# Dilated attention of a hybrid decoder step: pieces of one query block and four key blocks for both heads, set between half tiles of the projections

## What is computed

```python
def combine_branches(outs, lses):
    wts = jax.nn.softmax(jnp.stack(lses), axis=0)
    y = sum(wts[i][..., None] * outs[i] for i in range(len(outs)))

def dilated_prompt(q, k, v):
    for w, d in DIL_PATTERNS:          # (128,1), (512,4), (2048,16)
        o, lse = band_attn(sub(q), sub(k), sub(v), w // d)
```

## Time and profile before

| | |
|---|---|
| time, 3 runs | 3176.5 us median (3175.96 to 3176.5) |
| profiled execution | 3177.57 us, its span 3175.8 us |
| mean granted TensorE clock | 0.988 of full speed |
| TensorE matmul busy | 3010.7 us (95%) |
| VectorE, ScalarE, GpSimd busy | 1358.9 (43%), 655.0 (21%), 966.6 us (30%) |
| HBM traffic | 198 MB, 62 GB/s |

### The profile page before, as it was taken

One profiled execution on the slowest core, in us unless ns is written; L12 is line 12 of the kernel. 1 busy time (PEld: TensorE's weight loads), 2 busy tenths in 40 slices (PEclk: granted clock), 3 DMA queues, 4 the chain that ended last, 5 costly groups with the idle time before them and its releaser, 6 DMA issues. The chain is left out here.

```text
span 3175.8 us, 54540 instructions
## 1 busy us (share of the span) xinstructions
PE 3010.7 (95%) x20003; PEld 2855.9 (90%) x20003; DVE 1358.9 (43%) x2798; ACT 655.0 (21%) x1565; POOL 966.6 (30%) x989
## 2 busy tenths in 40 slices
PE   6999999999999999999889898999899999999996
PEld 5888988889999999999777776988799999999996
DVE  5555541254343444344733335522254434344436
ACT  3333321132000000002223335212221000000002
POOL 2222333423333333333311111343233333333331
PEclk9999999999999999999999999999999999999998
DMA  3101133311111111111122220233211111111111
GB/s 123 34 27 46 40 113 139 122 63 43 49 43 49 46 45 44 49 44 45 41 83 74 74 74 27 79 123 135 99 46 47 46 46 46 46 46 46 46 46 60
DMA packets 52491, 198.28 MB, mean 62 GB/s; under 512 B 6960, under 2 KB 14000, under 8 KB 49080
## 3 DMA queue, kind: packets, MB, share of 16 engines
q1 hardware_dynamic: 36912, 130.51, 12.3%
q10 hardware_dynamic: 15504, 66.71, 5.8%
HBM read 184.34 MB, written 13.10 MB: 62 GB/s over the span
## 5 line engine op out<-in xcount | busy, mean ns | idle before, releaser
L496 PE MATMUL linear<-h_hi,w_hi 128*128 128x344 f32 x3312 | 1075.2, 325 | 55.5 <-POOL w_lo L457 13.6
L496 PE MATMUL linear<-h_lo,w_hi 128*128 128x344 f32 x3312 | 1065.0, 322 | 0.0
L496 PE MATMUL linear<-h_hi,w_lo 128*128 128x344 f32 x3312 | 1064.6, 321 | 0.0
L452 POOL TENSOR_SCALAR w_hi<-w_raw 128x512 fp32r<-128x512 f32 x492 | 321.3, 672 | 2160.1 <-PE linear L496 2148.4
L496 PEld LDWEIGHTS linear<-h_hi,w_hi 128*128 128x128 f32 x3312 | 628.5, 190 | 66.6 <-issue 44.9
L457 POOL TENSOR_TENSOR w_lo<-w_raw,w_hi 128x512 fp32r<-128x512 f32 x492 | 654.3, 1353 | 0.0
L496 PEld LDWEIGHTS linear<-h_lo,w_hi 128*128 128x128 f32 x3312 | 628.3, 190 | 0.7 <-issue 0.2
L496 PEld LDWEIGHTS linear<-h_hi,w_lo 128*128 128x128 f32 x3312 | 628.6, 190 | 0.0
L1372 DVE TENSOR_TENSOR x<-linear,x 128x344 f32<-128x344 f32 x528 | 272.3, 516 | 211.2 <-PE linear L496 211.0
L496 PE MATMUL linear<-hid_hi,w_hi 128*128 128x344 f32 x1056 | 339.7, 322 | 5.0 <-DVE x L1372 5.0
L496 PE MATMUL linear<-hid_hi,w_lo 128*128 128x344 f32 x1056 | 340.0, 322 | 0.0
(11 more groups left out here) (209 smaller groups left out, 3145.2 us busy)
## 6 DMA issues: line engine op xcount, KB each, us to landing
w_raw<-in_w SPq DMA_DIRECT2D x246, 512.0 KB, 3.5
kv_slotc<-in_mem_cache_k ACTq DMA_DIRECT2D x8, 2048.0 KB, 8.4
kv_slotc<-in_mem_cache_v ACTq DMA_DIRECT2D x8, 2048.0 KB, 9.8
kv_slot<-in_dil_k ACTq DMA_DIRECT2D x4, 1536.0 KB, 7.5
kv_slot<-in_dil_v ACTq DMA_DIRECT2D x4, 1536.0 KB, 6.7
out_y<-answer ACTq DMA_DIRECT2D x6, 688.0 KB, 3.6
x<-in_x ACTq DMA_DIRECT2D x2, 1376.0 KB, 9.1
out_dil_k_out<-k ACTq DMA_DIRECT2D x4, 516.0 KB, 3.1
```

The costliest lines, as they stand in the source:

```text
L452: pool.tensor_scalar(w_hi[:, s, c], w_raw[:, s, c], 1.0, 0.0, ALU.mult, ALU.add).then_inc(pool_hi, 1)
L496: mm = pe.matmul(out, w[:, slot, cols], a, start=(k == 0 and j == 0), stop=(k == n - 1 and j == 2))
```

## The change

- The jobs become 12 **pieces** to a pair: one query block, both heads, at most four key blocks. Blocks 7 to 4 have two pieces (4 and 4, 3, 2, 1 key blocks), blocks 3 to 0 one (4, 3, 2, 1). Both heads are in every S, T and V.
- There is one score buffer, `ps_scores`, one half for each head. A second piece continues the running maximum of the first; the exponentials of both wait for the bias of the closing one. The row sums of two pieces are added.
- The rows are no longer multiplied by the reciprocal. Behind V of a closing piece TensorE makes a matmul of the reciprocals, broadcast to 64 columns, with the identity ("spread"), and VectorE copies it to `mix` and multiplies `ps_mixed` by it ("scale"), in place of ScalarE's copy.
- The two-turn loop is gone: four pairs are written out for TensorE, ScalarE and VectorE. The v unit of pair 0 comes first (`att1pre`); in pair i the units are q(i), k(i), v(i+1). Tables give the steps after each half tile: the last steps of pair i-1 in the q unit (DIL_DRAIN), the turning of the values (position 1) and S of piece 0 in the k unit (DIL_KEY), most of pair i in the v unit (DIL_FILL). The last pair has no v unit, so its DIL_FILL and DIL_DRAIN run with nothing between them.
- ScalarE loads the keys of pair i+1 behind the sample's V of pair i, and the values behind the sample's exponential, as before. The store of v is moved behind S of piece 9.
- A third buffer for rows lies in `mix`, or over `h_hi` for the last pair.

The diff, cut to its core (steps of the sample and the bookkeeping of the semaphores are left out):

```diff
-        "dil": [(qb, (h,)) for qb in range(QB - 1, 3, -1) for h in (0, 1)] + [(qb, (0, 1)) for qb in (3, 2, 1, 0)],
...
+PIECES = [(qb, 4 * part, min(4, qb + 1 - 4 * part), part == 0, 4 * part + 4 > qb)
+          for qb in reversed(range(QB)) for part in range(1 + qb // 4)]
+SAMPLE_S = 8
+SCORE_ORDER = list(range(SAMPLE_S)) + ["sample"] + list(range(SAMPLE_S, len(PIECES)))
+TURN_ORDER = list(range(len(PIECES))) + ["sample"]
+CLOSING = [k for k, piece in enumerate(PIECES) if piece[4]]
+BIAS_ORDER = [k for k in SCORE_ORDER if k == "sample" or PIECES[k][4]]
+DIL_KEY = {5: [("S", 0)]}
+DIL_FILL = {1: [("S", 1)],
+            2: [("S", 2), ("T", 0)],
+            3: [("S", 3), ("T", 1), ("V", 0), ("S", 4), ("T", 2), ("V", 1)],
+            4: [("S", 5), ("T", 3), ("V", 2), ("S", 6), ("T", 4), ("V", 3)],
+            5: [("S", 7), ("T", 5), ("V", 4), ("S", "sample"), ("T", 6), ("V", 5)],
+            6: [("S", 8), ("T", 7), ("V", 6), ("S", 9), ("V", 7), ("S", 10), ("T", 8), ("S", 11), ("T", 9), ("V", 8)]}
+DIL_DRAIN = {0: [("T", 10), ("V", 9)], 1: [("T", 11), ("V", 10)], 2: [("V", 11), ("T", "sample")], 3: [("V", "sample")],
+             4: [("R", "sample")]}
...
+def first_slot(phase):
+    return sum(turns * units for name, turns, units, _ in PHASES[:[p[0] for p in PHASES].index(phase)]) % 2
...
+        p1 = [[p1_ring[:, 0, :], p1_ring[:, 1, :], mix1[:, CH - 1, 0:1024] if i < PAIRS - 1 else p1_late[:, :]]
+              for i in range(PAIRS)]
...
-        score_banks = {kind: [(ps_s[:, :], ps_s[:, 512:1024]), (lin3[:, 0:1024], lin3[:, 512:1024])] for kind in ("dil", "mem")}
+        score_banks = {"mem": [(ps_s[:, :], ps_s[:, 512:1024]), (lin3[:, 0:1024], lin3[:, 512:1024])]}
...
-            with pe.Fori(0, PAIRS // 2) as i:
-                p = 0
-                for part in range(2):
-                    for u in range(3):
-                        p = unit("att1", i, 3 * part + u, p, TILES, h_hi, h_lo)
-
-                    pe.wait_ge(sem["freed_dve"], at("freed_dve", "att1", i, 9 * part + 6))
-                    attention("att1", i, "dil", q1, k1, vnat1, vnew1, qd1, p1, pt1, ps1,
-                              kv_slot1[:, :].rearrange("p (b n) -> p b n", b=BATCH_S),
-                              kv_slot1[:, :].rearrange("p (b m d) -> p b m d", b=BATCH_S, m=3), drawn1,
-                              [("freed_dve", at("freed_dve", "att1", i, 9 * part + 9))], part=part,
-                              turn_v=lambda: turn_values("att1", i, k1, v1, ("freed_dve", at("freed_dve", "att1", i, 9 * part + 9)),
-                                                         ("att1", i, part * (len(JOBS["dil"]) + 1))),
-                              slots=slot_value(1, 0, i, part))
...
+            unit("att1pre", 0, 0, 0, TILES, h_hi, h_lo, slot=first_slot("att1pre"))
...
+                def score(k):
+                    pe.wait_ge(sem["peaked"], at("peaked", ph, 0, SCORE_ORDER.index(k)))
...
+                        qb, kb, nb, _, _ = PIECES[k]
+                        pe.wait_ge(sem["freed_dve"], at("freed_dve", ph, 0, 5 if k == 0 else 6))
+                        for h in range(2):
+                            r = HEAD * h
+                            mm = pe.matmul(ps_s[:, 512 * h:512 * h + P * nb], q1[r:r + HEAD, P * qb:P * qb + P],
+                                           k1[r:r + HEAD, P * kb:P * kb + P * nb], start=True, stop=True)
+                    mm.then_inc(sem["scored"], 1)
...
+                def turn(k):
+                    pe.wait_ge(sem["exped"], at("exped", ph, 0, SCORE_ORDER.index(k) + 1))
+                    pe.wait_ge(sem["turned_in"], at("turned_in", ph, 0, TURN_ORDER.index(k)))
...
+                    qb, kb, nb, opens, closes = PIECES[k]
+                    if opens:
+                        pe.wait_ge(sem["scaled"], at("scaled", ph, 0, QB - 1 - qb))
+                    for m in range(nb):
+                        for h in range(2):
+                            r = HEAD * h
+                            mm = pe.matmul(ps_o[r:r + HEAD, 0:P], vnat1[:, kb + m, r:r + HEAD],
+                                           pt1[:, 512 * h + P * m:512 * h + P * m + P], start=(opens and m == 0),
+                                           stop=(closes and m == nb - 1), skip_group_check=True)
+                    mm.then_inc(sem["mixed"], 1)
+                    if closes:
+                        pe.wait_ge(sem["inverted"], at("inverted", ph, 0, BIAS_ORDER.index(k) + 1))
+                        c = 2 * (qb % 2)
+                        for h in range(2):
+                            r = HEAD * h
+                            mm = pe.matmul(ps_o[r:r + HEAD, P:2 * P], inv1[:, c + h:c + h + 1].to_broadcast([P, HEAD]), ident[:],
+                                           start=True, stop=True, skip_group_check=True)
+                        mm.then_inc(sem["spread"], 1)
...
+                drain(0)
+                p = unit(ph, 0, 0, 0, TILES, h_hi, h_lo, slot=slot, pause=lambda t: drain(2 * t + 1),
+                         after=lambda t: drain(2 * t + 2))
+                p = unit(ph, 0, 1, p, TILES, h_hi, h_lo, slot=1 - slot, pause=lambda t: key(2 * t + 1),
+                         after=lambda t: key(2 * t + 2))
+                if i < PAIRS - 1:
+                    unit(ph, 0, 2, p, TILES, h_hi, h_lo, slot=slot, pause=lambda t: fill(2 * t + 1),
+                         after=lambda t: fill(2 * t + 2))
+                else:
+                    for position in range(1, 7):
+                        fill(position)
+                last = step
+            for position in range(5):
+                drain(position)
...
-            with act.Fori(0, PAIRS // 2) as i:
...
+                    qb, kb, nb, opens, _ = PIECES[k]
+                    if opens and qb + 2 < QB:
+                        act.wait_ge(sem["inverted"], at("inverted", ph, 0, BIAS_ORDER.index(CLOSING[QB - 3 - qb]) + 1))
+                    for h in range(2):
+                        piece = p1[i][k % 3][:, 512 * h:512 * h + P * nb]
+                        c, d = 2 * (qb % 2) + h, 4 * (qb % 2) + (0 if opens else 2) + h
+                        mm = act.activation(piece, piece, ACT.Exp, scale=1.0 / 8.0, bias=bias1[:, c:c + 1],
+                                            accum_out=den1[:, d:d + 1])
+                    mm.then_inc(sem["exped"], 1)
...
+                def step(what, k):
+                    past_waits()
+                    if what == "S":
+                        if SCORE_ORDER.index(k):
+                            exponential(SCORE_ORDER[SCORE_ORDER.index(k) - 1])
+                        if k == 9 and i < PAIRS - 1:
+                            act.wait_ge(sem["freed_dve"], at("freed_dve", ph, 0, 9))
+                            act.dma_start(dram["dil_v_out"][i + 1], v1[:, :]).then_inc(stored["v"], 16)
+                    elif what == "T":
+                        act.wait_ge(sem["mixed"], at("mixed", ph, 0, TURN_ORDER.index(k)))
+                        act.wait_ge(sem["turned"], at("turned", ph, 0, TURN_ORDER.index(k) + 1))
+                        if k == "sample":
+                            copy(pt1[:, 0:384], ps_t[:, 0:384])
+                            mm = copy(pt1[0:BATCH_S, 384:512], ps_t[0:BATCH_S, 384:512])
+                        else:
+                            w = P * PIECES[k][2]
+                            mm = copy(pt1[:, :].rearrange("p (u n) -> p u n", u=2)[:, :, 0:w],
+                                      ps_t[:, :].rearrange("p (u n) -> p u n", u=2)[:, :, 0:w])
+                        mm.then_inc(sem["turned_in"], 1)
+                        if k == 9:
+                            exponential(SCORE_ORDER[-1])
...
-            with dve.Fori(0, PAIRS // 2) as i:
...
+                    qb, kb, nb, opens, closes = PIECES[k]
+                    dve.wait_ge(sem["turned"], at("turned", ph, 0, max(0, k - 2)))
+                    if not opens:
+                        dve.wait_ge(sem["peaked"], at("peaked", ph, 0, n))
+                    m = 1024 - P * (qb + 1 - kb)
+                    for h in range(2):
+                        c = 4 * (qb % 2) + h
+                        op = dve.tensor_tensor_reduce(p1[i][k % 3][:, 512 * h:512 * h + P * nb], ps_s[:, 512 * h:512 * h + P * nb],
+                                                      mask1[:, m:m + P * nb], 1.0, NEG if opens else peak1[:, c:c + 1],
+                                                      ALU.add, ALU.max, peak1[:, c:c + 1] if opens else peak1[:, c + 2:c + 3])
+                    op.then_inc(sem["peaked"], 1)
+                    if closes:
+                        if qb + 2 < QB:
+                            dve.wait_ge(sem["exped"], at("exped", ph, 0, SCORE_ORDER.index(CLOSING[QB - 3 - qb]) + 1))
+                        dve.wait_ge(sem["peaked"], at("peaked", ph, 0, n + 1))
+                        c = 4 * (qb % 2) + (0 if opens else 2)
```

(33 more changed lines are left out.)

227 lines of the change are left out of this document (195 added, 32 removed).

## The result

The changed kernel takes **3149.76 us** (median of 4 runs, 3147.91 to 3151.29); the kernel before, 3176.4 (3176.0 to 3176.5). The ratio is 0.9912, its 95% interval 0.990 to 0.9924. Five more runs beside the experiments gave 3149.24 against 3177.47. So it is 27 to 28 us faster; 21 were forecast, and the time lies in the range. The profiled execution took 3147.91 us with a span of 3146.1 us.

The account below looks back on a forecast made before the run. TensorE's own work was taken to bound the kernel. Gains of 15 (three pairs), 0.8 (last pair) and 4.8 us (loop's return) sum to 20.6 us off, about 3155.5 us from 3176.5; range 3137 to 3168.

Parts of the forecast that it names:

- the sum 38.2 + 2.0 + 5.6 = 45.8 us: A pair beside its units: TensorE work, gaps and waits, against 50.8 us before; 5.0 us less, 15 us for three pairs.
- The 9.6 us for V: TensorE's V work in one pair: 1.02, 0.81, 0.58, 0.37 us for pieces of 4, 3, 2, 1 key blocks.
- The 5.7 us for the sample's steps: Sample and turning of values in a pair, unchanged: 2.7 us S and values, 2.0 V, about 1.0 T and R.
- The 2.0 us of gaps: Second wait before each T and S, between 0 and 3.6 us a pair over 24 steps; 2.0 taken.
- The walked waits: TensorE's waits for VectorE and ScalarE in a woven pair, walked step by step from the v unit's start: 5.6 us together.
- The last pair: Chain without half tiles: ends 47.5 us behind its k unit, 50 us with S0, turning and gaps; gain 0.8 us.
- The loop's return: Goes with the two-turn loop: 3.3 us of delay and 1.5 us of slower matmuls; gain 4.8 us.
- Moved transfers: Moved loads of keys and values and stores: no gain or loss, bound 2 us the wrong way.
- The clock: Rival: lower clock through woven stretches, 33 us more each, chance 0.03. Separately, up to 4 us in last pair's tail, left out.
- The other engines set the pace: Rival: VectorE and ScalarE carry the v-unit stretch, half tiles hide nothing of their chain; 3168.5 us, chance 0.14.
- Fewer waits: Rival: waits and doubled gaps vanish in three pairs, 23 us more gain, 3133 us; chance 0.12.
- The heads don't run side by side: Rival: semaphores or the shared ps_mixed bank part the heads, S and V stay at 1.9 us; 3199 us, chance 0.02.

Follow-up runs that it names:

- V in the same columns: Changed kernel with V of both heads written to the same 64 rows of ps_mixed, so both use the same array columns: 3169.83 us, ratio 0.9975.
- S twice: Changed kernel with S of every piece issued twice for both heads, side by side, the second time with the same result: 3169.93 us, ratio 0.9972.
- the spread twice: Changed kernel with the spread of both heads issued twice, the second time with the same result: 3156.07 us, ratio 0.9926.
- the steps in two heaps: Changed kernel with all steps but S of piece 0 behind the v unit, and the drain in front of the next q unit: 3162.14 us.
- The version with more waits: Changed kernel with four more already met waits on TensorE before each S, T and V of the 12 pieces: 3150.8 us, ratio 0.9911.
- The two rearranged tables: Changed kernel with S 10, 11 and later steps moved into the next q unit: 3143.42 us; then also S 3, 5, 7, 8 one position earlier: 3137.5 us.
- the version with a table of its own: The second of the two rearranged tables, but with the last pair in the changed kernel's own order: 3135.37 us, ratio 0.9865.
- the version without the loop: Kernel before with only the phase's two-turn loop written out for TensorE, ScalarE and VectorE: 3173.66 us, ratio 0.9986.
- V head after head: Changed kernel with V of a piece doing all key blocks of head 0, then all of head 1: 3155.32 us, ratio 0.9925.
- S on the same rows: Changed kernel with S of both heads reading queries and keys of head 0, so both use the same array rows: 3183.96 us, ratio 1.0005.

## Why the prediction was right, and where a size was off

**TensorE's own work sets the pace, and side by side is what shrinks it: right.** V in the same columns costs 20.6 us, S twice 20.7, the spread twice 6.8. Work added to TensorE comes back in the time, less the part that falls in front of a wait. V was said to take 1.02 us throughout and takes 1.03 in front of an S. But the pieces bring waits of their own: with the steps in two heaps only 3.1 of the 7.2 us a pair are left, so the gain is side by side together with the half tiles that cover these waits.

**The mis-sized term is the sum 38.2 + 2.0 + 5.6 = 45.8 us for a pair beside its units.** The trace has 77.76 - 34.2 = 43.6, so 2.2 us a pair and 6.7 in three pairs were missing from the gain; that is nearly all of the gap between forecast and result. By its parts, for pair 1 (start to start, waits taken out):

| | forecast | measured |
|---|---|---|
| S | 10.2 | 10.4 |
| V | 9.6 | 8.9 |
| T | 9.7 | 9.35 |
| spread | 3.0 | 2.7 |
| sample and turning of values | 5.7 | 5.1 |
| gaps | 2.0 | 1.8 |
| waits | 5.6 | 5.25 |

- *The 9.6 us for V were a wrong reading of the right rows.* In the earlier trace rows the row behind such a V is a turn, and the distance includes the change from one kind of step to the other. Behind a closing V now stands the spread, a matmul of the same kind: 16 records 0.92 us, 12 0.70, 8 0.49, 4 0.27, against 1.02, 0.81, 0.58, 0.37 as taken. That is 0.1 us eight times a pair; the spread itself took 0.32, not 0.37.
- *The 5.7 us for the sample's steps* held "about 1.0" for two short turns that take 0.56, a number that could have been read.
- *The 2.0 us of gaps came out nearly right for a wrong reason.* I put them on the second wait of a T or S, 0.083 us each. The version with more waits prices a wait that is met at 4 ns. The gaps are at the breaks of the linear stream instead: 12 matmuls in front of a step take 2.0 to 2.1 us where 12 x 0.157 = 1.89 stand in an unbroken tile, and there are about 12 such breaks a pair.

**The walked waits: right as a whole, in position 6 partly by luck.** Forecast 5.6, measured 5.25. One by one, us: T0 0.5, 0.48; T2 1.05, 1.14; T4 0.9, 0.95; T6 0.2, 0.23; S9 0.5, 0.17; S10 0.8, 0.71; S11 1.15, 0.48; T10 0.5, 0.78; a wait at T9 of 0.30 wasn't in the walk. The four in front are right to 0.1; behind them too much at S9 and S11 (1.0 us) is half made up by T9 and T10. The two rearranged tables show that they were read rightly: moving just those steps that the waits named took away 2.06 and then 2.7 us a pair.

**The last pair:** 0.8 us forecast. From the first unit to R's end the phase fell from 344.6 to 316.7 us, so by 27.9; less 3 x 7.2 for the periods and 4.8 for the loop, 1.5 is left. The chain behind the k unit was walked at 47.5 us and took 47.2, nearer than the walk deserves: by the version with a table of its own, the same order without the lower clock is 0.9 us shorter (45.3 against 46.1 us from S1 to R), so the walk was some 1.2 us too long.

**The loop's return:** 4.8 us forecast; the version without the loop gives 4.84 us in the trace and 3.8, within its interval, in the time.

**Moved transfers:** no wait on a DMA stands among TensorE's, as forecast.

**The clock.** In the woven pairs it stayed at 1.00, as said. In the last pair it fell for some us, not in the tail of 12 us but in its head, behind a wait of 1.75 us:

```profile
1871.33 2.08 PE L862 MATMUL ps_scores<-k,q 64*128 64x512 f32 x4 [1.75 <-DVE peak L1841]
1873.34 1.60 PE L881 MATMUL ps_turned<-ident,p_ring 128*128 128x128 f32 x8
...
1876.21 1.07 PE L881 MATMUL ps_turned<-ident,p_ring 128*128 128x128 f32 x8 [0.32 <-ACT pt L988]
1877.20 1.09 PE L907 MATMUL ps_mixed<-pt,vnat 128*64 128x128 f32 x16
```

```profile
1870.00:1875.00 5.00, 3.64 (x14) 1.90 (x14) 2.75 (x9) 2.93 (x8) 0.00 (x0) 0.66 0.09 36
...
1904.00:1915.00 11.00, 7.54 (x130) 5.43 (x126) 2.48 (x10) 3.58 (x10) 0.00 (x0) 1.00 0.01 2
```

S2 takes 2.08 instead of 1.13 us and T0 1.60 instead of 1.09, 1.5 us in all; the chain lost less, 0.9 us, because a wait of T0 for ScalarE vanished in it. The tail, with TensorE busy 7.54 of 11 us in idle pieces of up to 0.8, keeps 1.00.

Other versions show that this is no single event. Of the twelve profiled executions without the loop and with pieces, nine have 3 us or more at the lower level in the head of the last pair, at the end of the same wait of 1.75 us (2.14 in one) or just behind it; V head after head, S twice and the table of its own have the wait and keep 1.00. The tail isn't safe either. In the version with two heaps it ends at the lower level, and in the one with more waits some 3 us of it lie right behind S9. The sample's V in the two heaps takes 2.71 us instead of 1.52:

```profile
1925.05 2.71 PE L896 MATMUL ps_mixed<-kv_slot,pt 128*32 128x128 f32 x48 [0.79 <-ACT pt L987]
```

```profile
1925.00:1930.00 5.00, 4.40 (x66) 3.11 (x66) 0.00 (x0) 0.39 (x3) 0.00 (x0) 0.52 0.00 0
```

The idle pieces in front of it are the same as in the changed kernel, 0.3 to 0.8 us. The Trainium skill (TensorE: Matmul & The Clock Gate, on psum-queue depth-cycling) let frequent short idles make the clock go back and forth; by that the tail would have cost up to 4 us. In the changed kernel's tail the trace doesn't bear it out, in the last pair of most other versions something like it happens. That it cost this kernel only 0.9 us is in part luck.

**The rivals.** "The other engines set the pace" falls with the spread twice and with the two heaps, though what half tiles hide (4.1 us a pair) and the part of added work that vanished in waits (a quarter of the spread's, a third of V's and S's) is its grain of truth. The Trainium skill (TensorEngine Tiling (Array Packing), PSUM Bottleneck) says that the emptying of PSUM may bound once tiling has sped up TensorE; here it sets single waits, 5.25 us in a period of 77.8, and not the pace. "Fewer waits" wasn't this kernel, but two tables later it was: 3135.4 us, where that rival said 3133. "The clock" didn't happen in the woven stretches here and did with S on the same rows. "The heads don't run side by side" falls: they do in one bank of `ps_mixed`, and even when issued head after head.

## What to carry to other kernels

Cost a step of the engine that bounds by the distance to a following row of the kind that will stand behind it in the new order, since the change from one kind of step to another has a price of its own (0.1 us here). Walk the chain of the other engines step by step and keep the list: each wait in it names a step that may stand half a tile earlier or later, and acting on the list gave half as much again as the change itself. An order that hides a latency behind other work can lengthen the chain where there is no such work (1.7 us here), so give the last turn a table of its own. Before a difference of 1 or 2 us is put down to an order, look whether the granted clock is the same in both traces.

## What the runs showed of the hardware

- Two heads' V in different columns overlap even when all of one head's records are issued first: 1.51 us for 16, against 1.03 in turn and 1.89 in the same columns.
- A wait that is already met costs TensorE about 4 ns on the average (144 in a pair, 0.64 us); a break in a stream of matmuls costs 0.1 to 0.2 us (12 matmuls take 2.0 to 2.1 us, not 1.89).
- Broadcast weights (64 columns from one) load at no visible extra cost: four records 0.32 us, eight 0.54.
- The granted clock fell to 0.54 for 13 us with TensorE busy 11.6 of them and no idle over 0.7 us, where S of both heads used the same 64 rows; with the same schedule on both halves it stayed at 1.00. With the heads' S on 64 rows in turn, as before the change, it stayed at 1.00 too.
- In a chain without half tiles a wait of 1.75 us (2.14 in one trace) was followed by, or ended in, 3 us or more at the lower level in nine traces; three stayed at 1.00.
